# Norms that follow their product bank by bank, and the last two gate products of each feed-forward layer side by side

## The reference, cut to what matters

```python
def rmsnorm(x, g):
    y = x * lax.rsqrt(jnp.mean(x * x, axis=-1, keepdims=True) + EPS)
    return y * g

# end of the first block
x = x + rms_norm(swiglu(rms_norm(x, g_pre_ffn), w_gu, w_down), g_post_ffn)
# second block; layer 0 is "fox", layer 1 is "mla"
for i in range(2):
    h = rmsnorm(x, norm_mix[i])
    p = h @ w_in[i]                                        # then the mixer -> o_mix, o_mem
    x = x + concatenate([o_mix, o_mem]) @ w_out[i]
    x = x + conv_ffn(rmsnorm(x, norm_ffn[i]), ...)         # gate and up products, a 3-tap
                                                           # convolution, silu, down product
```

## Time and profile before

| | us |
|---|---|
| median of three runs | 1459.53 |
| lowest, highest | 1458.98, 1460.73 |
| the profiled execution's own time | 1458.41 |
| its span | 1457.0 |
| PE busy | 1343.7 |
| DVE, ACT, POOL busy | 913.2, 686.4, 160.0 |

### The profile page before, as it was taken

How to read it: one execution, slowest core, us unless ns; L and a number is a source line. 1 busy time by engine, 2 the same in 40 slices (tenths; PEclk the granted TensorE clock), 3 DMA queues, 4 the chain that set the end, 5 groups by cost and what they waited for, 6 DMA issues and landing times.

```text
span 1457.0 us, 21408 instructions
## 1 busy us (share of the span) xinstructions
PE 1343.7 (92%) x8820; PEld 1206.9 (83%) x8820; DVE 913.2 (63%) x1303; ACT 686.4 (47%) x977; POOL 160.0 (11%) x262
## 2 busy tenths in 40 slices
PE   5999999999999989999997999899997769899997
PEld 5988899779978867899996777799996647799997
DVE  4456378887556546545546665677766577577675
ACT  4345455545434544544335454554454456454442
POOL 6000030040000000200000230000000261000000
PEclk9999999999999999999998999899998879999999
DMA  7431355423544425465564433365663320365661
GB/s 269 174 117 60 128 191 176 144 87 124 192 167 169 173 101 143 138 190 180 176 192 124 146 116 87 115 189 176 192 196 97 122 58 16 97 207 175 184 192 59
DMA packets 206400, 212.68 MB, mean 146 GB/s; under 512 B 7009, under 2 KB 151859, under 8 KB 206304
## 3 DMA queue, kind: packets, MB, share of 16 engines
q1 hardware_dynamic: 203840, 206.25, 44.2%
q0 software_dynamic: 2160, 4.02, 0.8%
q10 hardware_dynamic: 304, 1.05, 0.2%
HBM read 210.24 MB, written 1.05 MB: 145 GB/s over the span
## 4 chain that ended last, share of the span: by engine, by line
PE 66%; DVE 7%; ACT 4%; issue 1%; POOL 1%; DVEq 0%; ACTq 0%; POOLq 0%
PE psum_a L454 8%; PE psum_a L456 8%; PE psum_a L455 8%; PE psum_b L454 7%; PE psum_b L456 7%; PE psum_b L455 7%; PE psum_c L454 4%; PE psum_c L456 4%; PE psum_c L455 4%; DVE w_lo L444 2%; PE psum_c L572 2%; ACT w_hi L434 1%; DVE pair_peak L1595 1%; PE psum_c L2370 1%; ACT normed_rows L555 1%
## 5 line engine op out<-in xcount | busy, mean ns | idle before, releaser
L444 DVE TENSOR_TENSOR w_lo<-raw,w_hi 128x2048 fp32r<-128x2048 f32 (+3 forms) x235 | 449.9, 1950 | 87.9 <-ACT w_hi L434 87.0
L434 ACT ACTIVATE w_hi<-raw 128x2048 fp32r<-128x2048 f32 (+3 forms) x235 | 372.2, 1619 | 31.3 <-PE psum_b L456 16.7
L454 PE MATMUL psum_a<-x_hi,w_hi 128*128 128x256 f32 x752 | 215.6, 287 | 4.7 <-DVE w_lo L444 4.7
L454 PE MATMUL psum_b<-x_hi,w_hi 128*128 128x256 f32 x752 | 214.4, 285 | 0.8 <-issue 0.8
L455 PE MATMUL psum_a<-x_lo,w_hi 128*128 128x256 f32 x752 | 214.4, 285 | 0.0
L456 PE MATMUL psum_a<-x_hi,w_lo 128*128 128x256 f32 x752 | 214.3, 285 | 0.0
L455 PE MATMUL psum_b<-x_lo,w_hi 128*128 128x256 f32 x752 | 213.5, 284 | 0.0
L456 PE MATMUL psum_b<-x_hi,w_lo 128*128 128x256 f32 x752 | 213.5, 284 | 0.0
L454 PEld LDWEIGHTS psum_a<-x_hi,w_hi 128*128 128x128 f32 x752 | 146.4, 195 | 6.3 <-DVE w_lo L444 5.1
L455 PEld LDWEIGHTS psum_a<-x_lo,w_hi 128*128 128x128 f32 x752 | 146.1, 194 | 1.4
L454 PEld LDWEIGHTS psum_b<-x_hi,w_hi 128*128 128x128 f32 x752 | 145.0, 193 | 2.3 <-issue 0.9
(11 more groups left out here) (496 smaller groups left out, 2553.8 us busy)
## 6 DMA issues: line engine op xcount, KB each, us to landing
raw<-in_ffn_w_up_dram SPq DMA_DIRECT2D x88, 512.0 KB, 5.1
raw<-in_w_in_dram SPq DMA_DIRECT2D x40, 1024.0 KB, 5.5
raw<-in_w_gu_dram SPq DMA_DIRECT2D x44, 512.0 KB, 5.1
raw<-in_ffn_w_down_dram SPq DMA_DIRECT2D x44, 512.0 KB, 5.8
raw<-in_w_down_dram SPq DMA_DIRECT2D x22, 512.0 KB, 5.8
raw<-in_w_br_ssm_dram SPq DMA_DIRECT2D x8, 1024.0 KB, 5.0
raw<-in_w_xkv_dram SPq DMA_DIRECT2D x8, 1024.0 KB, 5.6
...
```

The lines of the kernel that those rows point to most:

```text
L434: act.activation(k.w_hi[:, s, 0:size], k.raw[:, s, 0:size], ACT.Copy).then_inc(*k.rounded.at(*key))
L444: dve.tensor_tensor(k.w_lo[:, s, 0:size], k.raw[:, s, 0:size], k.w_hi[:, s, 0:size].bitcast(F32), ALU.subtract).then_inc(*k.split.at(*key))
L454: pe.matmul(out_ap, l[0], r[0], start=start, stop=False, skip_group_check=True)
```

## The change

1. The list of pieces and PE's order at the end of each feed-forward layer: gate products 20 and 21 stand side by side, then come down products 19, 20 and 21.
2. The last down product of each layer, and the last part of the fox output product, signal each of their four banks (`part_made`); the fox part is reordered by row block (`pe_out_last`).
3. The sum into `res` and the squares go bank by bank (PARTS: row block 0 left and right half, then row block 1), all squares on ACT, and each row block has its own mean and its own root. DVE scales row block 0 and half of row block 1, ACT the other half. This holds for the norms `fox`, `ffn0` and `mla`; `ffn1`'s norm stays. The norm behind the first block's feed-forward goes the same way (`dve_post_parts`).
4. One weight piece less is split before the norms `fox` and `mla`; it is split behind `x_hi` and `x_lo` instead.
5. The output is stored in four transfers.

```diff
@@ weights, ffn()
             gate_up(0)
-            for h in range(1, FT):
+            for h in range(1, FT - 2):
                 gate_up(h)
                 down(h - 1)
-            down(FT - 1)
+            for h in (FT - 2, FT - 1):
+                gate_up(h)
+            for h in range(FT - 3, FT):
+                down(h)
@@ new functions
+PARTS = [(m, c) for m in range(MT) for c in range(2)]
+def act_norm_parts(k, tag, key):
+    for m, c in PARTS:
+        k.nc.scalar.wait_ge(*k.res_added.by(*key, m, c))
+        k.nc.scalar.activation(k.junk_rows[:, m, part(c)], k.res[:, m, part(c)], ACT.Square,
+                               accum_out=k.parts[:, 2 * m + c:2 * m + c + 1]).then_inc(*k.norm_sq_act.at(tag, m, c))
+def dve_norm_means(k, tag):
+    for m in range(MT):
+        dve.wait_ge(*k.norm_sq_act.by(tag, m, 0))
+        dve.tensor_scalar(x[:, 4 + m:5 + m], x[:, 2 * m:2 * m + 1], 1.0 / D, EPS, ALU.mult, ALU.add).then_inc(*k.norm_part.at(tag, m))
+        dve.wait_ge(*k.norm_part.by(tag, m))
+        dve.wait_ge(*k.norm_sq_act.by(tag, m, 1))
+        dve.scalar_tensor_tensor(...).then_inc(*k.norm_mean.at(tag, m))
+def pool_norm_roots(k, tag):
+    for m in range(MT):
+        pool.wait_ge(*k.norm_mean.by(tag, m))
+        pool.tensor_tensor(k.parts[:, 8 + m:9 + m], k.parts[:, 6 + m:7 + m], k.half_neg[:, 0:1], ALU.pow).then_inc(*k.norm_root.at(tag, m))
+def dve_norm_scales(k, tag):
+    dve.wait_ge(*k.norm_root.by(tag, 0))
+    dve.tensor_scalar(k.normed_rows[:, 0, :], k.res[:, 0, :], k.parts[:, 8:9], None, ALU.mult).then_inc(*k.scaled_dve.at(tag, 0))
+    dve.wait_ge(*k.norm_root.by(tag, 1))
+    dve.tensor_scalar(k.normed_rows[:, 1, 0:512], k.res[:, 1, 0:512], k.parts[:, 9:10], None, ALU.mult).then_inc(*k.scaled_dve.at(tag, 1))
+def act_norm_scales(k, tag):
+    act.wait_ge(*k.norm_root.by(tag, 1))
+    act.activation(k.normed_rows[:, 1, 512:1024], k.res[:, 1, 512:1024], ACT.Copy, scale=k.parts[:, 9:10]).then_inc(*k.scaled_act.at(tag))
+def pe_turn_parts(k, tag):
+    pe.wait_ge(*k.scaled_dve.by(tag, 0))
+    for j in range(4):
+        pe.transpose(quarter(k, j)[:, 0:P], k.normed_rows[:, 0, j * P:(j + 1) * P], k.ident[:])
+    pe.wait_ge(*k.scaled_dve.by(tag, 1))
+    for j in range(4):
+        pe.transpose(quarter(k, j)[:, P:2 * P], k.normed_rows[:, 1, j * P:(j + 1) * P], k.ident[:]).then_inc(*k.turned.at(tag, j))
+    pe.wait_ge(*k.scaled_act.by(tag))
...
+def dve_post_parts(k, tag, og, gain):
...
+    rows(0, 0)
+    begin(0)
+    rows(0, 1)
+    mean(0)
+    begin(1)
+    rows(1, 0)
+    mean(1)
+    add(0, 0)
+    rows(1, 1)
+    add(0, 1)
+    add(1, 0)
+    add(1, 1)
+def dve_add_parts(k, key, last):
+    for m, c in PARTS:
+        dve.wait_ge(*(k.part_made.by(*key, m, c) if (m, c) != (1, 1) else k.used.by(*last)))
+        r = k.res[:, m, part(c)]
+        dve.tensor_tensor(r, k.psum_c[:, D * m + 512 * c:D * m + 512 * c + 512], r, ALU.add).then_inc(*k.res_added.at(*key, m, c))
@@ pe_down
+            if h == FT - 1 and (m, n) != (1, 1):
+                mm.then_inc(*k.part_made.at(tag, m, n))
@@ pe_ffn
         pe_gate_up(k, tag, h)
-        pe_down(k, tag, h - 1)
-    pe_down(k, tag, FT - 1)
+        if h < FT - 2:
+            pe_down(k, tag, h - 1)
+    for h in range(FT - 3, FT):
+        pe_down(k, tag, h)
@@ act_ffn, and dve_ffn in the same way
-        act_split(k, 2)
+        act_split(k, 2 if h < FT - 1 else 1)
@@ dve_out, layer 0
+        for m, c in PARTS:
+            dve.wait_ge(*(k.used.by("out", layer, c, 0) if m else k.part_made.by("out", layer, m, c)))
+            dve.tensor_tensor(r, (k.psum_a, k.psum_b)[c][:, 512 * m:512 * m + 512], r, ALU.add).then_inc(...)
@@ scalar_program, and vector_program in the same way
-        act_norm_scale(k, tag, k.res)
+        act_norm_scales(k, tag)
         act_turn(k, tag, k.X, col["norm_mix_2"] + KD * layer)
+        act_split(k, 1)
         mixer(k)
...
-    for m in range(MT):
-        act.wait_ge(*k.res_added.by("ffn1", m))
-        act.dma_start(k.out[0, m * P:(m + 1) * P, :], k.res[:, m, :]).then_inc(*k.stored.at(m))
+    for m, c in PARTS:
+        act.wait_ge(*k.res_added.by("ffn1", m, c))
+        act.dma_start(k.out[0, m * P:(m + 1) * P, part(c)], k.res[:, m, part(c)]).then_inc(*k.stored.at(m, c))
```

More of the change, by code:

```diff
@@ new lines, in act_norm_scales @@
+def act_norm_scales(k, tag):
+    act = k.nc.scalar
+    act.wait_ge(*k.norm_root.by(tag, 1))
+    act.activation(k.normed_rows[:, 1, 512:1024], k.res[:, 1, 512:1024], ACT.Copy, scale=k.parts[:, 9:10]).then_inc(*k.scaled_act.at(tag))
+def pe_turn_parts(k, tag):
+    pe = k.nc.tensor
+    pe.wait_ge(*k.scaled_dve.by(tag, 0))
[5 more added lines that the diff above has]
+    pe.wait_ge(*k.scaled_act.by(tag))
+    for j in range(4, KD):
+        pe.wait_ge(*k.lo_made.by(tag, j - 4))
+        for m in range(MT):
+            mm = pe.transpose(quarter(k, j)[:, m * P:(m + 1) * P], k.normed_rows[:, m, j * P:(j + 1) * P], k.ident[:])
+        mm.then_inc(*k.turned.at(tag, j))
@@ new lines, in act_post_parts, with rows, begin, mean @@
+def act_post_parts(k, tag, last):
+    for m, c in PARTS:
+        k.nc.scalar.wait_ge(*(k.part_made.by(tag, m, c) if (m, c) != (1, 1) else k.used.by(*last)))
+        k.nc.scalar.activation(k.junk_rows[:, m, part(c)], k.psum_c[:, D * m + 512 * c:D * m + 512 * c + 512], ACT.Square,
+                               accum_out=k.parts[:, 10 + 2 * m + c:11 + 2 * m + c]).then_inc(*k.post_sq_act.at(tag, m, c))
+def dve_post_parts(k, tag, og, gain):
+    dve, x = k.nc.vector, k.parts
+    def rows(m, c):
+        dve.wait_ge(*k.post_sq_act.by(tag, m, c))
+        dve.tensor_tensor(og[:, m, part(c)], k.psum_c[:, D * m + 512 * c:D * m + 512 * c + 512], gain[:, part(c)],
+                          ALU.mult).then_inc(*k.post_gain_dve.at(tag, m, c))
+    def begin(m):
+        dve.wait_ge(*k.post_sq_act.by(tag, m, 0))
+        dve.tensor_scalar(x[:, 14 + m:15 + m], x[:, 10 + 2 * m:11 + 2 * m], 1.0 / D, EPS, ALU.mult, ALU.add).then_inc(*k.post_part.at(tag, m))
+    def mean(m):
+        dve.wait_ge(*k.post_part.by(tag, m))
+        dve.wait_ge(*k.post_sq_act.by(tag, m, 1))
+        dve.scalar_tensor_tensor(out=x[:, 16 + m:17 + m], in0=x[:, 11 + 2 * m:12 + 2 * m], scalar=1.0 / D, in1=x[:, 14 + m:15 + m],
+                                 op0=ALU.mult, op1=ALU.add).then_inc(*k.post_mean.at(tag, m))
+    def add(m, c):
+        dve.wait_ge(*k.post_root.by(tag, m))
+        dve.wait_ge(*k.post_gain_dve.by(tag, m, c))
+        dve.scalar_tensor_tensor(out=k.res[:, m, part(c)], in0=og[:, m, part(c)], scalar=x[:, 18 + m:19 + m], in1=k.res[:, m, part(c)],
+                                 op0=ALU.mult, op1=ALU.add).then_inc(*k.res_added.at(tag, m, c))
+    rows(0, 0)
[10 more added lines that the diff above has]
+    add(1, 1)
@@ L2579, in pe_fox @@
     pe.wait_ge(*k.o_lo.by(("fox", 7)))
-    for c in range(2):
-        take(outs[c], 1)
+    pe_out_last(k, 0, 3)
 def act_fox(k):
@@ L3109, in scalar_program @@
         if layer == 0:
-            act.wait_ge(*k.res_added.by("ffn0", 0))
-            act_norm(k, "mla", k.res)
-    for m in range(MT):
-        act.wait_ge(*k.res_added.by("ffn1", m))
-        act.dma_start(k.out[0, m * P:(m + 1) * P, :], k.res[:, m, :]).then_inc(*k.stored.at(m))
-    act.wait_ge(*k.stored.by(MT - 1))
+            act_norm_parts(k, "mla", ("ffn0",))
+    for m, c in PARTS:
+        act.wait_ge(*k.res_added.by("ffn1", m, c))
+        act.dma_start(k.out[0, m * P:(m + 1) * P, part(c)], k.res[:, m, part(c)]).then_inc(*k.stored.at(m, c))
+    act.wait_ge(*k.stored.by(MT - 1, 1))
 def vector_program(k):
@@ L3273, in gpsimd_program @@
     pool_ffn(k, "ffn")
-    pool_add_normed(k, "ffn")
-    pool_norm(k, "fox")
+    pool_post_roots(k, "ffn")
+    pool_norm_roots(k, "fox")
     pool_fox(k)
-    pool_norm(k, "ffn0")
+    pool_norm_roots(k, "ffn0")
     pool_ffn(k, "ffn0")
-    pool_norm(k, "mla")
+    pool_norm_roots(k, "mla")
     pool_mla(k)
```

80 lines of the change are left out of this document (52 added, 28 removed).

## The result

The kernel before took 1459.81 us (median of 4, 1458.98 to 1460.73) and the changed one **1443.09 us** (median of 4, 1441.62 to 1444.28), 16.7 us less: a ratio of **0.9885, interval 0.9868 to 0.9902**. Predicted were 1446.1. The changed kernel was run again later: 1442.94 us, ratio 0.9890 (0.9875 to 0.9905). One run of experiment 7 took 3344.7 us, where its other three lie between 1441.2 and 1444.5, and is left out of its median. The profiled execution took 1443.15 us with a span of 1441.8 us; before it was 1458.41 and 1457.0.

A forecast was written before the change was run, and what follows sets the result against it. PE, busy 1343.7 of 1457.0 us, was taken as the bound, with time only in its gaps and slow stretches. Gains of 13.9 less 0.5 for the clock gave 1445.0 profiled, 1446.1 us as median; range 1441.8 to 1451.0.

The forecast's parts named there:

- Gate products: Last down products of ffn0 and ffn1: the 2.05 us stall and the slow pass go, gaining 3.62 and 3.67 us.
- The shared buffer: Tiles 19 and 21: rounding waits for down product 19, no cost; rival: stall returns, 1453.4 us, chance 0.02.
- The norms: Norms fox, ffn0 and mla: `x_hi` earlier by 2.6, 0.95 and 1.9 us; rival of no gain 1451, chance 0.10.
- The first block's end: Norm ahead of fox: `x_hi` at T + 7.95 instead of T + 10.56, gain 2.6 us, bounds 2.0 and 3.2.
- The end: Behind ffn1's last matmul: sums end 1.7 us earlier, stores save 0.65, gain 2.3 us, bounds 1.7 and 2.4.
- the fixed point: ffn0's norm: DVE's split ends at T - 1.0 in both versions, T being PE's last matmul's end before the gap.
- The moved piece: Fox's wait before the first scores grows by 1.15 us, bounds 0.5 and 2.0; in mla cost 0 (to 0.5).
- The rival of the weight stream: Fox and mla: a weight piece lands after it is wanted and later ones are late too: 1460.5 us, chance 0.03.
- The clock: PE's earlier restarts in three places: a few matmuls at level 0.50, 0.5 us off; clock rival 1449.3, chance 0.13.
- more gain: Rival: with shorter gaps the clock doesn't fall before ffn0 and mla, 1.5 us each: 1443 us, chance 0.10.

The follow-up runs named there:

- experiment 7: Changed kernel with the weight piece behind fox's output product split only behind ffn0's `x_hi` and `x_lo`: 1443.13 us (median of three).
- 10: Changed kernel with mla's second weight piece split ahead of its norm again, as in the kernel before: 1447.01 us.
- 11: Changed kernel with eight more (repeated) transposes on PE in front of mla's `x_hi`: 1443.25 us.
- experiment 6: Kernel of experiment 4 with four more (repeated) transposes on PE in front of fox's `x_hi`: 1444.01 us.
- 4: Changed kernel with fox's second weight piece (1072 columns) split ahead of the norms again, mla's left behind: 1447.18 us.
- 5: Changed kernel with eight more (repeated) transposes on PE in front of fox's `x_hi`: 1446.85 us.
- 1: Kernel before with the gate products side by side and the moved weight piece, but the old norms: 1453.50 us.
- 2: Changed kernel with the old order of gate and down products and the old place of the weight piece: 1454.06 us.
- 8: Changed kernel with the norms' scaling shared by row block, ACT all of row block 0, DVE all of row block 1: 1446.72 us.

## Why the prediction was right, and where it was not

**Gate products.** Right. Forecast 3.62 and 3.67 us, measured 3.91 and 3.74 (`x_hi` to T in ffn0, 195.87 to 191.96; the cut in ffn1), and 3.97 and 3.79 with this part alone. The last pass runs at full clock, with no wait ahead; the changed kernel's stretches in the first block and in ffn0:

```profile
777.40:780.37 2.97, 2.97 (x13) 2.06 (x11) 1.84 (x4) 2.03 (x6) 0.00 (x0) 1.00 0.34 72
1102.40:1105.36 2.96, 2.96 (x13) 2.06 (x11) 2.96 (x3) 0.30 (x1) 0.00 (x0) 1.00 0.00 0
```

**The shared buffer.** Right: only in the first block did POOL's rounding wait for down product 19, and no matmul waited for the rounding.

**The norms.** The first block's end 3.09 us against 2.6 and mla 2.05 against 1.9. The end 2.44 against 2.3. In ffn0 0.95 was forecast, with `x_hi` at T + 4.8; it starts at T + 6.21. The gain itself was there, 1.12 us from the end of DVE's split (911.69 to 918.43 before, 907.78 to 913.40 after). What failed is the fixed point: I took the split to end at T - 1.0 "in both versions", and it ended at T + 0.6. Without a half level ahead of T, the last output products took less time and T came forward against the split. In experiments 10 and 11, with 3.4 us at half level ahead of T again, `x_hi` starts at T + 4.65 and 4.63, close to the forecast's 4.8. Experiment 7 shows that split as the whole hold-up.

**The moved piece.** Right: from `x_hi` to the scores 0.99 us longer, 1.25 by experiment 6, against 1.15; waits of 0.58 + 3.40 = 3.98 us against 4.2; no cost in mla (134.31 for 134.29 us with the products alone, which move the piece), no wait for a transfer in either. The rival of the weight stream is out.

**The clock.** This is the term that was mis-sized: -0.5 us, thought of as a few matmuls behind shorter gaps. The trace gave +3.2 in fox (3.17 shorter where 0.2 longer was forecast, less the 0.2 by which ffn0's norm did better) and -2.0 in mla, and in the start the first block's T came 1.2 us later, 1.1 of it in code that didn't change. The forecast had asked whether the level lasts into the restart behind the gaps that the change shortens. It does so in mla, for about 1.0 us by itself. It left out the waits that the change only moves: fox's wait, 0.3 us longer and with another of 0.58 ahead of it, stopped bringing the clock down. Experiments 4 and 6 have the same fox program with the wait 0.6 us apart against the slow stretch ahead, and 3.05 us of difference; that the position decides is the reading that fits them and experiments 10 and 11, and what sets it isn't known.

The two errors had opposite signs, and that they left the total inside the range is luck. Of the 3.0 us by which the median lies under the forecast, 1.8 are of the stages (15.2 us between the two profiled executions instead of 13.4). The other 1.2 are the 1.1 that I added because the profiled execution of the kernel before lay that far under its median; the changed kernel's lies on it (1443.15 and 1443.09). My rival "more gain" named 1443 and the clock, but for a reason that isn't what happened: the level still fell at ffn0 and at mla.

**What stays open.** Which waits bring the clock down was forecast right once (experiment 6), half right once (5: 3.4 us for 6.8), and for mla not at all; I have no rule that gives it from a trace. Up to the `x_hi` of the first block's feed-forward all kernels have the same code, and it takes 585.8 to 588.7 us, with 29 to 40 us at half level, not in step. Why was not tried. Against the changed kernel this adds 0.6 to 1.6 us to the profiled executions of experiments 1, 2, 4, 8 and 10, and takes 1.0 and 1.3 from those of 5 and 11, so differences of their medians aren't their edits alone. None of the variants was faster than the changed kernel.
